# Two weight stages of the first block: every second modulation unit's low part moves from GpSimd to VectorE

## The reference, cut to what matters

```python
def second_block(...):
    for l in range(DEPTH):
        mod_lat = (silu_c @ ada_w[l] + ada_b[l])[:, None, :]
        mod_ctx = silu_cc @ ada_w[l] + ada_b[l]
        sh1, sc1, g1, sh2, sc2, g2 = jnp.split(mod_lat, 6, axis=-1)
```

## Time and profile before

| | |
|---|---|
| median of 3 runs | 3329.77 us (3327.42 to 3330.16) |
| profiled execution | 3327.57 us, span 3325.7 us |
| PE busy | 3010.1 us, 91% |
| POOL busy | 2194.7 us, 66% |
| ACT busy | 1478.9 us, 44% |
| DVE busy | 1275.0 us, 38% |
| mean granted TensorE clock | 0.927 |

### The profile page before, as it was taken

One profiled execution on the slowest core, in us unless ns is written; L12 is line 12 of the kernel. 1 busy time (PEld: TensorE's weight loads), 2 busy tenths in 40 slices (PEclk: granted clock), 3 DMA queues, 4 the chain that ended last, 5 costly groups with the idle time before them and its releaser, 6 DMA issues.

```text
span 3325.7 us, 50132 instructions
## 1 busy us (share of the span) xinstructions
PE 3010.1 (91%) x21088; PEld 2719.3 (82%) x21088; DVE 1275.0 (38%) x1965; ACT 1478.9 (44%) x1918; POOL 2194.7 (66%) x912
## 2 busy tenths in 40 slices
PE   7999989989989899798988987988979979789898
PEld 7887779978778699695988976855979978469898
DVE  2455330134553311446224333665123336642333
ACT  5654544446545444453433443433434444344343
POOL 6677778876777788572675865640857867238486
PEclk9998989999999899896999988976989999789899
DMA  6445445554454455442344544420535554125354
GB/s 211 148 158 171 160 165 184 183 180 143 154 174 159 161 184 184 147 165 89 134 158 140 181 137 170 145 99 1 184 121 175 182 172 147 56 70 178 108 190 140
DMA packets 134721, 499.47 MB, mean 150 GB/s; under 512 B 15072, under 2 KB 15712, under 8 KB 133088
## 3 DMA queue, kind: packets, MB, share of 16 engines
q1 hardware_dynamic: 131904, 480.53, 43.0%
q10 hardware_dynamic: 2592, 15.73, 1.3%
HBM read 490.96 MB, written 5.24 MB: 149 GB/s over the span
## 4 chain that ended last, share of the span: by engine, by line
PE 77%; DVE 9%; ACT 5%; issue 2%; DVEq 2%; POOL 2%; ACTq 1%; DMA 1%; SPq 0%
PE lin L392 17%; PE lin L393 17%; PE lin L394 17%; PE aux L392 3%; PE aux L394 3%; PE aux L393 3%; PE lin L757 3%; PE aux L464 2%; ACT whi L857 2%; POOL wlo L371 2%; PE aux L777 1%; DVE Z L1239 1%; PE lin L418 1%; PE lin L419 1%; PE lin L420 1%
## 5 line engine op out<-in xcount | busy, mean ns | idle before, releaser
L371 POOL TENSOR_TENSOR wlo<-raw,whi 128x1024 fp32r<-128x1024 f32 x908 | 2194.5, 2433 | 1114.1 <-ACT whi L857 1113.3
L857 ACT ACTIVATE whi<-raw 128x1024 fp32r<-128x1024 f32 x908 | 948.2, 1057 | 1073.1 <-PE lin L394 885.6
L392 PE MATMUL lin<-in_hi,whi 128*128 128x256 f32 x4160 | 1208.4, 290 | 74.2 <-issue 31.2
L393 PE MATMUL lin<-in_lo,whi 128*128 128x256 f32 x4160 | 1192.2, 287 | 0.0
L394 PE MATMUL lin<-in_hi,wlo 128*128 128x256 f32 x4160 | 1191.2, 286 | 0.0
L392 PEld LDWEIGHTS lin<-in_hi,whi 128*128 128x128 f32 x4160 | 812.3, 195 | 87.1 <-issue 86.8
L393 PEld LDWEIGHTS lin<-in_lo,whi 128*128 128x128 f32 x4160 | 812.3, 195 | 4.1 <-issue 3.3
L394 PEld LDWEIGHTS lin<-in_hi,wlo 128*128 128x128 f32 x4160 | 811.1, 195 | 0.0
L392 PE MATMUL aux<-br_hi,whi 128*128 128x256 f32 x880 | 249.5, 284 | 7.6 <-DVE br_lo L1239 7.6
L393 PE MATMUL aux<-br_lo,whi 128*128 128x256 f32 x880 | 249.2, 283 | 0.0
L394 PE MATMUL aux<-br_hi,wlo 128*128 128x256 f32 x880 | 249.2, 283 | 0.0
(11 more groups left out here) (227 smaller groups left out, 3633.8 us busy)
## 6 DMA issues: line engine op xcount, KB each, us to landing
raw<-in_wstream SPq DMA_DIRECT2D x908, 512.0 KB, 3.3
kv_store<-Z ACTq DMA_DIRECT2D x2, 2048.0 KB, 8.5
Z<-kv_store ACTq DMA_DIRECT2D x2, 2048.0 KB, 10.5
Z<-in_rel ACTq DMA_DIRECT2D x2, 1536.0 KB, 7.5
Z<-in_mem_t ACTq DMA_DIRECT2D x2, 1024.0 KB, 6.9
x<-in_x_t SPq DMA_DIRECT2D x1, 1024.0 KB, 4.8
Z<-in_ctx_t SPq DMA_DIRECT2D x1, 1024.0 KB, 4.6
out_x<-x SPq DMA_DIRECT2D x1, 1024.0 KB, 3.9
```

Source lines behind the costliest of these rows:

```text
L371: pool.tensor_tensor(wlo[s][:, :], raw[s][:, :], whi[s][:, :].bitcast(F32), ALU.subtract).then_inc(lo_pool, 1)
L392: pe.matmul(out, wh, xh, start=start, stop=False, skip_group_check=True)
L393: pe.matmul(out, wh, xl, start=False, stop=False, skip_group_check=True)
L857: act.activation(whi[s][:, :], raw[s][:, :], ACT.Copy).then_inc(hi_ready, 1)
```

## The change

In the modulation chunks of the attention stage (0 to 4) and of the memory stage (5, 6, 7) of both layers the low parts of the second and the fourth unit are made by DVE. These are 2 x 8 x 2 = 32 of 908 units. `n_dve` is replaced by the set `on_dve`, and the semaphore values that SP and PE wait for are counted for each engine (`dve_made`, `pool_made`). DVE's `lo_part()` calls stand where they stood; 32 of them now issue a wait for the unit's high part and a subtraction of 128 x 1024.

```diff
+        def modulation(c):
+            on_dve.extend((len(units) + 1, len(units) + 3))
+            chunk(ada, c * CH)
+
...
             if isinstance(c, tuple):
                 chunk(w_in, GATE_COL + c[0] * D + c[1] * CH)
             else:
-                chunk(ada, c * CH)
+                modulation(c)
...
         for c in ADA_XA:
-            chunk(ada, c * CH)
+            modulation(c)
...
-def build(nc, a, n_units, n_first, n_dve):
+def build(nc, a, n_units, n_first, on_dve):
+
+    dve_made = list(accumulate(int(i in on_dve) for i in range(n_units)))
+    pool_made = [i + 1 - m for i, m in enumerate(dve_made)]
...
-                if 0 <= freed < n_dve:
-                    sp.wait_ge(lo_dve, freed + 1)
+                if freed in on_dve:
+                    sp.wait_ge(lo_dve, dve_made[freed])
                 elif freed >= 0:
-                    sp.wait_ge(lo_pool, freed - n_dve + 1)
+                    sp.wait_ge(lo_pool, pool_made[freed])
...
-            for i in range(n_dve, n_units):
+            for i in range(n_units):
+                if i in on_dve:
+                    continue
                 s = i % SLOTS
                 pool.wait_ge(hi_ready, i + 1)
                 pool.tensor_tensor(wlo[s][:, :], raw[s][:, :], whi[s][:, :].bitcast(F32), ALU.subtract).then_inc(lo_pool, 1)
...
             def lo_part():
                 i = n[0]
                 n[0] += 1
-                if i < n_dve:
+                if i in on_dve:
                     s = i % SLOTS
                     dve.wait_ge(hi_ready, i + 1)
                     tt_(wlo[s][:, :], raw[s][:, :], whi[s][:, :].bitcast(F32), ALU.subtract).then_inc(lo_dve, 1)
```

More of the change, by code:

```diff
@@ L2 @@
 from contextlib import ExitStack
+from itertools import accumulate
 import numpy as np
@@ L79, in stream @@
 def stream(v):
-    units = []
+    units, on_dve = [], []
     def unit(w, blocks, width):
@@ L153, in stream @@
         second(l)
-    return np.concatenate(units, 0), first
+    return np.concatenate(units, 0), first, frozenset(on_dve)
 class Count:
@@ L384, in next_unit @@
                 n[0] += 1
-                if i < n_dve:
-                    pe.wait_ge(lo_dve, i + 1)
+                if i in on_dve:
+                    pe.wait_ge(lo_dve, dve_made[i])
                 else:
-                    pe.wait_ge(lo_pool, i - n_dve + 1)
+                    pe.wait_ge(lo_pool, pool_made[i])
                 return whi[i % SLOTS], wlo[i % SLOTS]
@@ L1971 @@
                           + [tiles(v["subln_g_2"]), conv, taps, tiles(v["ada_b_2"])], -1)
-    weights, n_first = stream(v)
+    weights, n_first, on_dve = stream(v)
     data = dict(
@@ L1987 @@
     args["kv_store"] = nc.dram_tensor("kv_store", (L * P, 16 * T), F32, kind="Internal").ap()
-    build(nc, args, len(weights) // P, n_first, 0)
+    build(nc, args, len(weights) // P, n_first, on_dve)
     r = run_kernel(nc, [{f"in_{n}": np.ascontiguousarray(w) for n, w in data.items()}], core_ids=[0])
```

## The result

The changed kernel takes 3352.81 us on the median (3349.76 to 3355.02, four runs), the kernel before 3329.38 us on the same chip: the ratio is 1.0071 [1.0053, 1.0088] (in brackets here and below the 95% interval), 23.4 us slower. Its profiled execution took 3354.14 us with a span of 3352.0 us.

What follows compares the result with a forecast made beforehand. The prediction took PE as the bound, with DVE's queue as the path where modulation units make PE's work short. 16.8 us a layer, 33.6 in both, plus 5 for the clock gave 38.6 us more: 3367 us, range 3341 to 3390.

Steps and rivals of the forecast that it cites:

- the term for the clock: About ten lengthened idle stretches lower the granted clock, 0.5 us each: 5 us more, between 0 and 15.
- The prize: PE's first loads of modulation units waited for POOL's low parts 6 times: at most 3.3 us to gain.
- Chunk 0: Attention stage: both subtractions fall into DVE's idle time, cost 0 with 0.1 us to spare.
- Chunks 1 and 2: Attention stage: high-part waits and subtractions delay `gate_inverse`, `lowest` and PE's values by 3.15 us in each chunk.
- Chunks 3 and 4: Attention stage: 3.2 us for the first pair, 4.1 us at chunk 4, its last subtraction covered; 7.3 us together.
- Memory stage: Late `divide(0)` and later subtractions cost 4.7 us, earlier loads give back 1.5: net 3.2 us a layer, bounds 0 and 5.
- The sum without the clock: Attention and memory stage delays, 16.8 us a layer, add up to 33.6 us over both layers.
- The lock: DVE and POOL's shared port: subtractions meet POOL in four places a layer; all 32 meeting it would add 69 us.
- POOL was the limit: Rival, whole kernel: POOL bounds it, so the change gains at most 6.3 us, 3321 to 3325 us; chance 0.06.
- Absorbed: Rival: PE's dense gate units behind each place take up the delay, 3329 to 3334 us; chance 0.09.
- Only the long stages: Rival: chunks 1 and 2 cost a third, or the memory stage zero: 3343 to 3350 us; chance of less 0.15.
- Locked and slow: Rival: subtractions meet POOL in most places, clock falls in every lengthened stretch: 3385 to 3395 us; chance of more 0.08.

Runs made afterwards that it cites:

- middle first: Changed kernel with DVE's work for the chunk before (`gate_inverse`, `modulation_bias`) put ahead of the second low part, in both stages: 3322.66 us.
- both orders: Changed kernel with DVE's work for the chunk before ahead of the subtraction and each layer's last attention `gate_inverse` put behind that stage: 3323.95 us.
- the changed kernel with the gate deferred: Changed kernel with the last `gate_inverse` of each layer's attention stage put behind that stage, nothing else moved: 3323.62 us.

## Why the prediction was right

The forecast was 3367 us, range 3341 to 3390, slower with 0.85. Direction and mechanism came out; the figure was 14 us too high, and the step that failed is the term for the clock. That the sum of the other terms came out within 1 us is partly luck, since two misses in it cancel (chunks 1 to 3 too dear, the last subtraction of chunk 4 too cheap).

- **The prize.** At most 3.3 us, off the critical path. Nothing of it came (3.2 us are left). POOL's busy time fell by 72.7 us where 77 were forecast: the other 876 low parts became longer by 4 to 5 us together (2438 against 2433 ns, mean).
- **Chunk 0.** Forecast 0. The interval of row minima across its two subtractions is 12.13 us in both kernels.
- **Chunks 1 and 2.** Forecast 3.15 us each, measured 2.52 and 2.53 (2.82 and 2.53 in layer 1). The steps are the forecast ones, one by one: pass at 0.69 us, reciprocal 3.36 us later instead of 3.6, PE's values moved by exactly what `lowest(13)` was moved. The sum ran high because each hand-over from one DVE instruction to the next was priced at its full length, where the rows overlap by about 0.1 us.
- **Chunks 3 and 4.** Forecast 3.2 + 4.1 us, measured 2.53 + 4.03. The last subtraction was held covered; its interval grew by 1.3 to 1.5 us, so the cover that the forecast took for granted was not there. The attention stage was to grow by 13 to 16 us a layer; on PE it grew by 16.0 and 14.3, by the yardstick 12.9 and 13.4.
- **Memory stage.** Forecast 3.2 us a layer, measured on the queues 3.3 (6.5 in both). The gain inside it came as well: ACT's last high part no longer waits for a load, but for PE:

```profile
441.89 1.06 ACT L868 ACTIVATE whi<-raw 128x1024 fp32r<-128x1024 f32 x1 [1.18 <-PE lin L524]
...
420.27 0.66 PE L660 MATMUL aux<-c,probs 128*128 128x128 f32 x4 [3.21 <-DVE probs L1586]
...
443.47 1.05 PE L533 MATMUL lin<-c,ytok 4*128 4x2 f32 x8 [0.83 <-ACT ytok L925]
```

  PE waits 3.21 us for `divide(0)`, where it was 0.86. On PE the stage hardly grew, from 46.64 to 47.49 us in layer 0: the transposes of the result row took 1.05 instead of 1.86 us. The delay was there and the clock paid it back: in this stage and just behind it, it stood at half for 6.8 us before and for 3.4 us after. With the memory stage's half of the change alone it stood at half for 10.2 us there (layer 0), and the time rose by 9.1 us.
- **The sum without the clock.** Forecast 33.6 us, measured 26.3 + 6.5 = 32.8 on DVE's and ACT's queues, and PE is 33.4 us late at unit 630.
- **The clock, the term that was mis-sized.** Forecast 5 us more, between 0 and 15, on the ground that longer idle stretches mean more time at half speed. What is left in its place is 23.4 - 32.8 = -9.4 us, a difference between medians and one profile's queues, not a measurement of the clock. What the profiles show is two things. The fall that was forecast came: ahead of unit 630 the clock stood at half for 304 to 307 us in the three profiles with the attention stage changed and DVE's order as it was, for 266 to 280 us in the four with its code as before. Yet PE is there only 0.6 us later than the queues say, so by this sum it cost next to nothing there, where DVE's queue was the path. And in one piece of the second block, which the change does not touch, 6.6 and 13.8 us were given back in the two profiles of the changed kernel. The bound of 0 from below was wrong: I had looked for places where the clock could fall, and not for places where it was low already, 92 us in that piece, and could rise.
- **The lock.** Four subtractions a layer meet POOL in chunk 4 and the memory stage (2.54, 2.53, 2.06 and 2.55 us in layer 0), as forecast; a fifth, the first of the memory stage, touches it (1.68 us). All 32 take 49.6 us where 32 x 1.22 would be 39.0, so the lock cost 10.6 us of DVE time. The Trainium skill (SBUF — State Buffer, on the two sides of SBUF) says that the second to start is blocked until the first is over. The rows agree (POOL 278.47 to 280.83, subtraction to 281.91, 1.08 us behind, near its own 1.22). The 69 us of meeting POOL each time did not come about, since DVE mostly waited for ACT until POOL was through.

**The rivals.** "POOL was the limit" is out: PE waited as long for POOL's low parts as before, and the one wait that went (ACT's for a load, 0.96 us in layer 0) was outweighed in its own stage. "Absorbed" is out by the intervals. "Only the long stages" gives a total near the measured one (3343 to 3350) for the wrong reason, since chunks 1 and 2 cost all but 0.6 us of what was forecast. "Locked and slow" had both of its surcharges wrong.

**What stays open.** The piece between units 630 and 650 took 161.8 to 169.1 us in six profiles of the four kernels in which all 32 low parts are DVE's, and 175.6 to 175.9 us in eight profiles of the other eight kernels. That the two groups do not overlap speaks against pure chance; what sets it is open. A later arrival alone does not (the two kernels with added work at the start, up to 33 us, did not get the shorter time), and neither half of the change does. The medians of middle first, of both orders and of the changed kernel with the gate deferred lie 12 to 23 us under what their queues give. This piece makes 6.6 to 11.6 us of that in their profiles; the rest is open, and I don't claim that gain for the order.

## What to carry to other kernels

Moving work from a fuller engine that hardly anyone waits for to an emptier one that stands on the chain made this kernel slower, by what was put in front of the chain's next step; read who waits for the engine before asking how full it is. Where moved work must go into such a queue, its wait counts beside its length (7.8 and 15.7 us of the attention queues here), so put it behind the work that the chain needs: that gave back 17 of 26 us. A long instruction in front of a result that others wait for is the first thing to look for: taking one `gate_inverse` a layer from there gained 0.5%, more than any placement of the low parts.

## What was not expected of the hardware

- The granted clock is at half in long stretches of one piece of the second block, and not in the same ones in every profile. The windows view of the kernel before, at full clock, then at half:

```profile
2195.00:2204.90 9.90, 4.82 (x22) 3.66 (x20) 8.67 (x7) 7.04 (x7) 5.66 (x3) 1.00 0.19 68
2205.00:2259.00 54.00, 46.50 (x104) 24.58 (x105) 28.04 (x64) 13.76 (x35) 3.73 (x2) 0.50 0.09 29
```

  PE was busy for 4.82 of 9.90 us before the clock fell from 2.4 to 1.2 GHz, and it stayed there for 54 us. In the changed kernel it fell at nearly the same point of the program, at 2238.19 us instead of 2204.94, but was back at full after 24 us:

```profile
2238.30:2262.00 23.70, 16.08 (x30) 7.66 (x31) 13.62 (x31) 5.54 (x14) 3.86 (x2) 0.50 0.19 67
2262.20:2272.00 9.80, 8.14 (x35) 4.27 (x33) 5.60 (x15) 4.02 (x10) 0.00 (x0) 1.00 0.00 0
```

- A wait can shorten what stands behind it: the pass over 128 x 1024 takes 1.63 us beside POOL and 0.69 us once POOL is through, so 3.28 us of waiting moved the next row minimum by 0.25 us.
